# Activation sums at three offsets, and down-projection weights at another, against each other in a four-sublayer macaron trunk

## The reference

```python
def swiglu(h, w_gate, w_up, w_down):
    return (jax.nn.silu(h @ w_gate) * (h @ w_up)) @ w_down
...
    for layer in range(DEPTH):
        x = x + 0.5 * swiglu(rmsnorm(x, norm_gain[layer, 0]), ...)
        h = rmsnorm(x, norm_gain[layer, 1])
        x = x + mixer(h)
        x = x + 0.5 * swiglu(rmsnorm(x, norm_gain[layer, 2]), ...)
    return rmsnorm(x, final_gain)
```

## Time and profile before

| what | value |
|---|---|
| median of three executions | 1998.66 us (1996.43 to 2000.04) |
| the profiled execution | 1998.84 us |
| its span, first to last instruction | 1996.9 us |
| granted TensorE clock over the span | 0.997 |
| PE, DVE, ACT, POOL busy, share of the span | 99%, 69%, 49%, 26% |
| mean DMA rate | 100 GB/s |

### The profile page before, as it was taken

The page is one execution under the profiler, slowest core; times in us unless marked ns, Lnnn a source line. Parts: engine busy times, 40 slices in busy tenths (PEclk is TensorE's granted clock), DMA queues, the critical chain, the costliest instruction groups (busy, mean ns, idle before and its releaser), DMA issues.

```text
span 1996.9 us, 30677 instructions
## 1 busy us (share of the span) xinstructions
PE 1967.4 (99%) x12159; PEld 1733.6 (87%) x12159; DVE 1386.3 (69%) x1928; ACT 978.3 (49%) x1472; POOL 516.9 (26%) x530
## 2 busy tenths in 40 slices
PE   9999999999999999999999999999999999999998
PEld 7898998787788988998898999878888888989996
DVE  6964977588647955973894696376766558946963
ACT  5543653445645633653562464355564555524642
POOL 1201311454221301311130221157566111302311
PEclk9999999999999999999999999999999999999999
DMA  5232332444122232332233223222222122332331
GB/s 189 94 129 85 106 130 72 121 130 135 54 85 95 106 118 83 110 126 82 95 114 104 90 107 125 72 77 96 69 77 92 53 95 95 114 108 85 117 127 43
DMA packets 63167, 199.95 MB, mean 100 GB/s; under 512 B 12816, under 2 KB 14896, under 8 KB 63024
## 3 DMA queue, kind: packets, MB, share of 16 engines
q1 hardware_dynamic: 59616, 196.55, 29.2%
q10 hardware_dynamic: 3408, 1.44, 0.3%
HBM read 188.51 MB, written 2.38 MB: 96 GB/s over the span
## 4 chain that ended last, share of the span: by engine, by line
PE 87%; DVE 6%; ACT 3%; issue 2%; POOL 1%; DMA 1%; ACTq 0%; SPq 0%; DVEq 0%; POOLq 0%
PE prod L590 16%; PE prod L592 15%; PE prod L591 15%; PE misc L684 6%; PE misc L685 6%; PE misc L686 6%; PE prod L684 4%; PE prod L685 4%; PE prod L686 4%; PE misc L905 2%; DVE h_lo L1619 1%; ACT L1443 0%; ACT h_hi L1156 0%; PE misc L784 0%; PE prod L980 0%
## 5 line engine op out<-in xcount | busy, mean ns | idle before, releaser
L590 PE MATMUL prod<-h_hi,p_hi 128*128 128x512 f32 x728 | 300.6, 413 | 2.2 <-DVE p_lo L1503 1.3
L592 PE MATMUL prod<-h_hi,p_lo 128*128 128x512 f32 x728 | 285.3, 392 | 0.0
L591 PE MATMUL prod<-h_lo,p_hi 128*128 128x512 f32 x728 | 284.4, 391 | 0.0
L590 PE MATMUL prod<-a_hi,d_hi 128*128 128x512 f32 x693 | 273.3, 394 | 0.0
L591 PE MATMUL prod<-a_lo,d_hi 128*128 128x512 f32 x693 | 272.8, 394 | 0.0
L592 PE MATMUL prod<-a_hi,d_lo 128*128 128x512 f32 x693 | 272.6, 393 | 0.0
L1503 DVE TENSOR_TENSOR d_lo<-raw,d_hi 128x1408 fp32r<-128x1408 f32 x64 | 104.0, 1626 | 240.1 <-ACT d_hi L1070 240.0
L2100 POOL TENSOR_TENSOR s_f<-raw 128x512 f32<-128x512 f32 x70 | 94.4, 1348 | 675.0 <-DVE s_lo L1578 361.9
L1070 ACT ACTIVATE d_hi<-raw 128x1408 fp32r<-128x1408 f32 x64 | 88.4, 1381 | 227.1 <-PE prod L592 226.5
L1503 DVE TENSOR_TENSOR p_lo<-raw,p_hi 128x1024 fp32r<-128x1024 f32 x86 | 111.6, 1298 | 77.4 <-ACT p_hi L1070 77.1
L590 PEld LDWEIGHTS prod<-h_hi,p_hi 128*128 128x128 f32 x728 | 137.2, 188 | 31.0 <-issue 8.5
(11 more groups left out here) (371 smaller groups left out, 5267.7 us busy)
## 6 DMA issues: line engine op xcount, KB each, us to landing
raw<-in_w SPq DMA_DIRECT2D x252, 512.0 KB, 3.4
raw<-in_wd SPq DMA_DIRECT2D x64, 704.0 KB, 4.2
blk<-blocks SPq DMA_DIRECT2D x16, 256.0 KB
x<-in_x SPq DMA_DIRECT2D x8, 256.0 KB, 5.9
k_dup<-k_dup SPq DMA_DIRECT2D x8, 256.0 KB, 3.5
silu_g<-g_rows SPq DMA_DIRECT2D x7, 256.0 KB, 4.8
out<-y_out SPq DMA_DIRECT2D x12, 128.0 KB, 1.9
raw<-in_w SPq DMA_DIRECT2D x4, 256.0 KB, 6.0
```

Of the source, the lines that this page charges most:

```text
L590: pe.matmul(bank, wh, hi, start=k == 0, stop=False)
L591: pe.matmul(bank, wh, lo, start=False, stop=False)
L592: ins = pe.matmul(bank, wl, hi, start=False, stop=k == tiles_n - 1)
```

## The change

The three first sums get steps of 32, 128 and 64 bytes ahead of them (a fourth of 32 makes 256), so t0 to t3 lie at 32, 160, 224 and 0 modulo 256 instead of 0. Against their weights, at 64, that is 224, 96, 160 and 192 instead of 192. `T_ROOM` grows by 256, which keeps `t_lo` at the same residues as `t_hi` and moves the tiles behind by 512 bytes. The wide views move to 0; the old place of the third stays as a fourth, and `weights` gives it to the last down unit of an FFN's first half.

```diff
 W_SHIFT = 64
-T_ROOM = 4 * KT // 2 * TOKENS * 4
+T_STEP = (8, 32, 16, 8)
+T_ROOM = (4 * KT // 2 * TOKENS + 64) * 4
...
         wide = [tuple(w_part(f"d_{part}{i}", at + HALF * P * 4 * j, HALF * P) for j, part in enumerate(("hi", "lo")))
-                for i, at in enumerate((2 * W_SHIFT, 4 * QB + 2 * W_SHIFT, 14 * QB + 3 * W_SHIFT))]
+                for i, at in enumerate((0, 4 * QB + ALIGN, 14 * QB + ALIGN, 14 * QB + 3 * W_SHIFT))]
...
             if is_down(n):
+                if n == down_unit(f, 0, KT - 1):
+                    return wide[3]
                 return wide[2 if u % 2 else 1 - ab_place(f, FT - 1)]
...
         t_hi, t_lo, t_f = ([nc.alloc_sbuf_tensor_at(f"{n}{i}", [P, KT // 2, TOKENS], dt, offset=t_at + part * T_ROOM
-                                                    + i * KT // 2 * TOKENS * 4) for i in range(4)]
+                                                    + (i * KT // 2 * TOKENS + sum(T_STEP[:i + 1])) * 4) for i in range(4)]
```

## The result

The changed kernel takes 2001.98 us in the median of 18 executions (2000.86 to 2004.79), against 1997.98 for the kernel before in the same comparison (18 executions): a ratio of 1.002, interval 1.0013 to 1.0027, 4.0 us slower. The profile after was taken of one such execution.

What follows compares the result with a forecast made beforehand. The prediction took TensorE's (PE's) matmul stream as the bound. Down weights -9.5, sums 0 and residue changes +1.1 gave -8.4 us, from 1998.8 to 1990.4 us; the range was 1984.5 to 1999.

Steps and rivals of the forecast that it cites:

- the down weights: Down-projection units: moved to residue 0 they would take 7.48 us each, saving 9.5 us in all.
- The rival that the residue isn't the cause: Down units: something other than residue slows them, so no gain, 1998.8 to 1999.9 us; chance 0.07.
- what I drew from a rule of the Trainium skill: TensorE's operand ports are independent, so relative offset is worth nothing and time would stay at 1998.8 us.
- The final unit: Split last down unit, 256 columns: 66 matmuls gain 0.3 or lose 0.1 us at residue 0; taken as 0.
- The activation sums: Fast stage: three sums moved from residue 192 to 224, 96 and 160 stay at 113.3 ns a matmul; cost 0.
- my three slow rows with 256 columns: Final unit at residue 64, 117.8 ns; index products at 0, 120 ns; one product at 192, 117.5 ns.
- The upper bound: Fast stage: shifted sums at the slower pace lose 4.4 ns a matmul, 3.7 us a sum, 11.1 for three.
- the rival of slow sums: Fast stage: one, two or three shifted sums take 117.7 ns, giving 1994.1, 1997.8 or 2001.5 us; chance 0.17.
- the corner that my range left out: Fast stage: part of the case of three slow sums, 2001.5 us, beyond the range's upper end of 1999.
- The changes of residue: Fast pairs: four added residue changes a pair, 280 in all, at 4 ns each cost 1.1 us.
- The spreading pace: Fast stage: residue changes set off a slow pace nothing ends, 5880 matmuls paying 4.4 ns, 25.9 us, 2015; chance 0.07.

Runs made afterwards that it cites:

- the map: Kernel before with sums t0, t1, t2, t3 at residues 0, 32, 64, 128 and down weights as before: 2015.01 us in one execution.
- the last run: Kernel before with down units at 0, first halves' m = 7 at 128, s43 weights of each FFN's second fast pair 160 bytes further: 1990.1 us.

## Why the prediction was wrong, point by point

**The bound, and the down weights: right.** PE's stream was the whole matter, and the residue of weights against activations sets its pace. I asked for 7.48 us a unit and 9.5 us in all; the unit takes 7.48 and the eight halves give 9.3. The rival that the residue isn't the cause is out. So is what I drew from a rule of the Trainium skill (TensorE: Matmul & The Clock Gate, Part 2: What happens when you issue a matmul), that the offset of the two operands is worth nothing: with no instruction changed, the same matmul took 113.3 to 119 ns by address alone. Whether it is the loading of the next weights that takes from the running matmul, no run here shows.

**The final unit: right within its bounds.** I took 0; 51 of its matmuls, from 1980.97 to 1987.08 us after, take 119.8 ns instead of 117.8, about 0.1 us lost.

**The activation sums: the step that failed.** I put 0 for three sums, because the same tiles at 192 sat at 113.3 and 17/16 of a cycle per column, met at two residues, looked like a floor of the stream. A floor it may be: no run went below. That it can be reached at one residue is no sign that it is reached at others, and of my three slow rows with 256 columns two were at other residues, while the third showed that 192 itself has a slow pace. In place of 0 the runs show about 5 ns for each of the 2520 matmuls, 11.8 us for the sums alone and 12.8 us lost in the fast stage. The upper bound, 11.1 us for three sums at 117.7, was the value to take. I chose the value nearest in tile and shape, where the change moved the very thing that told the rows apart. So the rival of slow sums, to which I gave 0.17, came true with all three slow, the corner that my range left out. Its 2001.5 beside the measured 2001.98 is partly luck: it leaves out the slow pace that the new down units hand over, and stays near only because the sums end that pace.

**The changes of residue: right in size, as far as it can be read.** I took 1.1 us for four changes in a pair. Only the one back to 192 can be read apart: the h product behind t1 is 16 ns longer (1.38 against 1.36 us, at the rows' rounding 20), 1.1 us over 70 pairs. The other three are part of what the sums take.

**The spreading pace: it exists, but I had its cause the wrong way round.** I gave 0.07 to a slow pace at 192 that nothing ends, set off by the shifted sums. The pace exists and does hold a whole half: but it is the down units of the half before that hand it over, with those ahead at 0 and the last at 0 or 64, and it is the shifted sums that end it in the first pair. So the sums cost 12 us alone, and within the change they also save what the down weights alone lose in the fast stage: 16 us in the second halves, up to 20 with the first halves. The two parts had to be read as one, and I priced them apart.

## What to carry to other kernels

Where PE never waits, look at the distance of matmul starts, not at busy time: PE is 99% busy in both kernels, while over many matmuls the distance shows to the nanosecond what an address costs. A stretch that runs at the best pace at one relative address says nothing about another, so when a change moves that address, take the slow rows as the forecast and the fast row as the hope. And before moving the operands of one stage, check in what pace it leaves the next one: here moving four of the 64 down units, the last ahead of each second half, from residue 64 to 128 was worth 16 us of 2000 (104.73 against 108.83 us in each second half).

## What the runs showed of the hardware

A stream of float32r matmuls with new weights for each has more than one stable pace at the same addresses. At residue 192 with 256 columns these are 113.3 and 117.8 ns; either was held for 924 matmuls, and a product at another residue ended the slow one. With 512 columns, residue 0 came back to 226.7 ns whatever went before in these traces; 64 ran at 229 or 233.3 (odd units of the earlier trace rows), 128 at 232 to 233, 192 at 233.3. Which pace a stretch falls into depended on more than the unit just ahead: two units at the very same addresses left one pace behind six units at 0, and the other behind six at 64 and 128. The runs agree with a pace that goes by the distance of the two operands and not by the address of one, at the three distances that were reached in two ways. At 32, twelve matmuls take 1.40 us with the moving operand shifted (t1 of the map) and with the weights shifted (the last run's s43 products, which start at 668.69 and 670.09 us, the next at 671.48). At 0, a matmul takes 118 to 119 ns with both at 64 (t0 of the map) and 119.8 with both at 0 (the final unit after). At 64, it takes about 118 ns with the weights at 64 (t2 of the map) and 117.8 with them at 192.

What conflicts, why 192 should be the good distance for 256 columns and 0 for 512, and what in the units ahead chooses the pace, no run here shows. Distances were counted modulo 256 throughout; another modulus was not tried, nor steps finer than 32 bytes.
